# Spreading the next phase's H between the last two pairs of a phase, in a gather-and-sum trunk on one core

## What is computed

```python
def chunk_fn(args):
    hc, ic, gc = args                                # 128 tokens: h, 128 indices, 128 gates each
    act = jnp.einsum('cd,ckd->ck', hc, u_tab[ic])    # the "dots"
    return jnp.einsum('ck,ckd->cd', gc * jax.nn.gelu(act), v_tab[ic])   # the "sums"
```

## Time and profile before

| | us |
|---|---|
| median of 3 runs | 1794.7 (1791.46 to 1794.89) |
| the profiled execution | 1795.44 |
| its span in the trace | 1793.6 |

### The profile page before, as it was taken

How to read it: one execution, slowest core, us unless ns; L and a number is a source line. 1 busy time by engine, 2 the same in 40 slices (tenths; PEclk the granted TensorE clock), 3 DMA queues, 4 the chain that set the end, 5 groups by cost and what they waited for, 6 DMA issues and landing times.

```text
span 1793.6 us, 17530 instructions
## 1 busy us (share of the span) xinstructions
PE 1289.4 (72%) x5712; PEld 537.7 (30%) x5712; DVE 1126.5 (63%) x2528; ACT 663.7 (37%) x1983; POOL 623.6 (35%) x559
## 2 busy tenths in 40 slices
PE   3676545657876996897778789789987975545555
PEld 2364011112621333333336133353352620000000
DVE  8957989883558666435445766654453577676454
ACT  6524332222234328216423331751382243233222
POOL 5103334452232224324422322332332344444442
PEclk9897667889876998999989699899998986787676
DMA  7039899999997999999999899999999999999996
GB/s 313 1 123 397 337 423 413 409 407 419 422 423 304 409 423 419 425 423 421 422 423 423 337 367 425 421 367 420 423 378 411 422 349 421 410 417 413 420 422 282
DMA packets 88652, 685.29 MB, mean 382 GB/s; under 512 B 12144, under 2 KB 12272, under 8 KB 14320
## 3 DMA queue, kind: packets, MB, share of 16 engines
q0 software_dynamic: 73728, 536.90, 73.2%
q1 hardware_dynamic: 14832, 147.26, 19.7%
HBM read 683.08 MB, written 1.05 MB: 381 GB/s over the span
## 4 chain that ended last, share of the span: by engine, by line
DMA 35%; PE 33%; DVE 17%; ACT 6%; issue 5%; POOL 3%; SPq 1%; POOLq 0%; ACTq 0%; DVEq 0%
DMA ringmem<-experts,lay 24%; PE ps L437 11%; PE ps L407 10%; DMA wt<-w_qkv 7%; DVE ringmem L1068 6%; PE ps L447 4%; POOL ringmem L1039 3%; DMA wt<-w_o 2%; PE ps L422 2%; ACT lay L773 1%; DMA wt<-w_q 1%; ACT S L724 1%; PE ps L626 1%; PE ps L601 1%; PE ps L513 1%
## 5 line engine op out<-in xcount | busy, mean ns | idle before, releaser
L1039 POOL DMA_INDIRECT ringmem<-experts,lay x512 | 588.2, 1149 | 1084.4 <-PE ps L407 946.5
L407 PE MATMUL ps<-ringmem,S 128*32 128x512 f32 x2048 | 626.8, 774 | 393.8 <-ACT S L724 393.4
L1068 DVE CUSTOM_DVE_ANT_0 ringmem<-ringmem,Hrep 128x1024 f32<-128x1024 f32 x512 | 614.6, 1224 | 310.1 <-DMA ringmem<-experts,lay 300.6
L407 PEld LDWEIGHTS ps<-ringmem,S 128*32 128x32 f32 x2048 | 115.0, 128 | 817.4 <-ACT S L724 565.9
L719 ACT ACTIVATE gelus<-dots 128x2 f32<-128x2 f32 x256 | 51.6, 202 | 693.1 <-DVE dots L1068 692.2
L437 PE MATMUL ps<-wt,hT 128*128 128x512 f32 x576 | 256.2, 598 | 13.6 <-DMA wt<-w_qkv 13.5
L437 PEld LDWEIGHTS ps<-wt,hT 128*128 128x128 f32 x576 | 106.6, 190 | 163.3 <-issue 155.0
L715 ACT ACTIVATE S<-con,lay 128x32 f32<-128x32 f32 x512 | 134.3, 310 | 35.9 <-PE ps L407 35.8
L724 ACT ACTIVATE S<-S,gelus 128x32 f32<-128x32 f32 x512 | 136.9, 314 | 23.7
L447 PE MATMUL ps<-hT,wt 128*128 128x128 f32 x1024 | 119.8, 279 | 2.6 <-DMA wt<-w_q 1.5
L447 PEld LDWEIGHTS ps<-hT,wt 128*128 128x128 f32 x1024 | 117.1, 194 | 14.5 <-issue 6.3
(11 more groups left out here) (187 smaller groups left out, 1116.0 us busy)
## 6 DMA issues: line engine op xcount, KB each, us to landing
wt<-w_qkv SPq DMA_DIRECT2D x36, 2048.0 KB, 11.6
wt<-w_q SPq DMA_DIRECT2D x16, 2048.0 KB, 12.0
wt<-w_glu SPq DMA_DIRECT2D x5, 2048.0 KB, 12.5
ringmem<-experts,lay POOLq DMA_INDIRECT x512, 12.6
wt<-w_o SPq DMA_DIRECT2D x4, 2048.0 KB, 13.8
ringmem<-w_glu SPq DMA_DIRECT2D x3, 2048.0 KB, 17.1
gain<-gains SPq DMA_DIRECT2D x9, 512.0 KB, 15.0
area<-keys SPq DMA_DIRECT2D x4, 1024.0 KB, 9.6
```

The costliest lines, as they stand in the source:

```text
L407: last = pe.matmul(ps[TG * t:TG * (t + 1), half, :], S[:, u % 2, i, :], ring[:, (2 * u + i) % RING, D + half * 512:D + (half + 1) * 512], ...
L1039: pool.indirect_dma_start(ring[:, s % RING, :], None, experts[phase // NC], bass.IndirectOffsetOnAxis(ap=rows[:, phase % NC, j, n:n + 1], ...
L1068: last = v.tensor_tensor_reduce(ring[:, i, 0:D], ring[:, i, 0:D], Hrep[:, j, :], 1.0, 0.0, ALU.mult, ALU.add, dots[:, b, second:second + 1])
```

## The change

The same instructions run on every engine; only their order on PE, ACT and DVE is another, at the ends of phases 0, 1 and 2.
- PE puts two spread pieces (u = 0, 1) ahead of the sums of pair 63, two (u = 2, 3) ahead of those of pair 64, and four behind.
- ACT copies the first four pieces between its shares of pair 63 and of pair 64 (`g.at` at u = 0 runs up to pair 63, at u = 4 up to pair 64), the last four behind. The root comes behind all eight and behind ACT's share of the next pair 1.
- DVE does the dots of the next pair 1 ahead of the addition to `X`.

```diff
@@ PE, spread_h
                 pe.wait_ge(normed, norm_event(phase // NC, phase % NC, 1) + 1)
                 for u in range(2 * QUAD):
+                    if phase and u in (0, 2, 4):
+                        g.at(phase - 1, PAIRS_G - 2 + u // 2)
                     j, half = divmod(u, 2)
@@ PE, the phases
             layer0(0, 1)
-            g.at(0, PAIRS_G)
             spread_h(1)
             layer1(1, 0)
-            g.at(1, PAIRS_G)
             spread_h(2)
             layer1(2, 1)
-            g.at(2, PAIRS_G)
             spread_h(3)
             g.at(3, PAIRS_G)
@@ ACT, spread_h
-                if phase:
-                    act.wait_ge(dots_ready, PAIRS_G * phase)
                 for u in range(2 * QUAD):
                     j, half = divmod(u, 2)
+                    if phase and u in (0, QUAD):
+                        g.at(phase - 1, PAIRS_G - 1 + u // QUAD)
+                        act.wait_ge(dots_ready, PAIRS_G * phase - 1 + u // QUAD)
                     act.wait_ge(h_spread, 2 * QUAD * phase + u + 1)
                     act.copy(Hrep[:, j, half * 512:(half + 1) * 512],
                              ps[:, src[u % len(src)], :]).then_inc(hrep_ready, 1)
-                    if e is not None and u == 3:
-                        root(e)
+                if e is not None:
+                    g.at(phase, 1)
+                    root(e)
@@ DVE, peer_end
                 c = phase % NC
                 g.at(phase, PAIRS_G)
+                if phase + 1 < 2 * NC:
+                    g.at(phase + 1, 1)
                 v.wait_ge(v_pe, PAIRS_G * (phase + 1))
                 v.tensor_tensor(X[:, c, :], X[:, c, :], banks(0, 2), ALU.add).then_inc(peer_done, 1)
```

## The result

| | before | after |
|---|---|---|
| median of 20 runs | 1793.6 us | 1798.6 us |
| ratio, with its 95% interval | | 1.0024 (1.0014 to 1.0034) |
| span of the profiled execution | 1793.6 us | 1797.0 us |

The change makes the kernel 4.3 us slower (2.5 to 6.1, the ratio on 1794). I had forecast 8.6 us slower. The direction was right, the size was not, and the parts were further off than their sum: the ends of phases 0 and 1 cost nothing together, the end of phase 2 costs more than all I had given it.

The account below looks back on a forecast made before the run. Bound by a chain of waits shared between transfers (35%) and PE (33%), DVE third. Phase ends 0, 1 and 2 cost 4.6, 1.7 and 2.3 us, together +8.6 (3.7 to 13.4): 1803.3 us for a 1794.7 median, range 1790 to 1811.

Parts of the forecast that it names:

- The late root: Ends of phases 0 and 1: scaling starts 3.7 us behind the last spread piece, +3.6 us at each end.
- DVE full, so a shift passes on: Ends of phases 0 and 1: DVE is full behind the scaling, so nothing covers the +3.6 us per end.
- Rival 3: DVE has slack, only the next pair 1's release counts: together -1.2 us, 1793.5, no change; chance 0.07.
- The wait for ACT ahead of pair 64's sums: ACT's share of pair 64 stands behind the fourth copy, so PE idles about 2 us before those sums.
- The spread's end at the ends of phases 0 and 1: Last spread piece ends +1.0 us at phase 0's end and -1.9 at phase 1's, middles over the open clock.
- Rival 2: Two high-clock stretches at each of the first two ends, sums and pieces being mixed: 1792.8, no change; chance 0.17.
- The end of phase 2: PE is already full there: spread ends +2.3 us (0.2 to 4.3), all on the chain through waiting gathers.
- DVE's dots ahead: Next pair 1's dots move between idle stretches of DVE, done before pair 64's sums: nothing on the chain.
- The late gathers: Gathers behind the last two pairs go out up to 6 us later, but DMA is full, so nothing starves.
- rival 4: The late gathers starve the stream, 3 us more at each end: 1812 us; chance 0.05.

Follow-up runs that it names:

- the delayed root: Kernel before, with the root behind all copies and ACT's share of the next pair 1, plus ten unneeded ACT copies ahead of it; 18.6 us slower.
- the kernel with the end of phase 2 alone: Changed order kept only at the end of phase 2, ends of phases 0 and 1 as in the kernel before; 6.1 us slower than before.
- the inner root: Changed order at ends of phases 0 and 1, root behind the sixth copy, phase 2's end as before: 9.5 us faster; with DVE's dots behind, 5.2 faster.

## Why the prediction was right or wrong

- **The late root: right.** I had the scaling 3.7 us behind the spread's end; it came 3.5 behind at both ends (547.31 to 550.81). The kernel with the root put back was 6.6 us faster, of 6.8 expected. The single comparisons scatter (3.8, 6.6, about 9 and 0 us for two ends). At one end the spread's end moved by up to 2.2 us from profile to profile of one order, with the granted clock, which may be the reason but is not shown to be; that a shift passes on in full rests on the delayed root.
- **DVE full, so a shift passes on: right.** Rival 3 is excluded by the delayed root, and gathers of the next pair 1 that came 6.5 us earlier brought nothing that the time shows.
- **The wait for ACT ahead of pair 64's sums: right,** 1.82 us.
- **The spread's end at the ends of phases 0 and 1: wrong, the term that failed.** I took +1.0 and -1.9 between all at the low clock and one stretch of high clock. From the end of pair 64's dots to the spread's end it was 15.1 us before at both ends, and 12.1 and 11.7 after: -3.0 and -3.4. My list for the end of phase 0 gave 10.5 us to the first four pieces and the sums of pair 63, at the low clock; they took 5.7, because the high clock fell on them, some 7 us of it instead of 3.4. It is not one lucky profile: from the start of pair 64's second dot to the spread's end it takes 14.2 to 17.0 us in ten ends with the old order (five kernels), 16.0 in the mean, and 11.2 to 13.4 in ten ends with PE's and ACT's new order (five kernels), 12.6 in the mean. Rival 2, to which I gave 0.17, has twice the time at the high clock, and its arithmetic for these two ends (0.4 and -2.5) fits the measured 0.4 and 0.0 better than mine (4.6 and 1.7). Its reason, that sums and pieces are mixed, is not shown: the kernel with the end of phase 2 alone, which has the old order here, was granted the high clock at the same place, while PE had little to do (stretches as above).

```profile
528.60:535.60 7.00, 2.59 (x12) 0.52 (x12) 3.16 (x6) 1.90 (x8) 4.25 (x4) 0.99 1.01 420
```

  What the new order changes is that PE has four pieces to do in such a stretch. My middle took the clock only around the eight pieces of the old place.
- **The end of phase 2: right in sign, too small.** +2.3 (0.2 to 4.3) against 6.1. I priced the sums of pair 63 at 1.98, since the clock was high at that time before. In the new order it stayed low, so pieces and sums cost 3.8 and 3.6. And I misread: the 12 matmuls in 3.65 us there are the eight of pair 62 and four of pair 63. The sums of both stood back to back and took 4.77 us, so those of pair 63 added 1.1 us and not the 1.98 of my sum; with pieces on both sides they cost 3.6. The new wait was in my sum and came (1.82).
- **DVE's dots ahead:** nothing on the chain in the changed kernel, as forecast (they end at 540.3, the root at 550.6). With the inner root it was not settled.
- **The late gathers: right at the first two ends, wrong at the third.** At the end of phase 0 the DMA share stays at 1.01 until 548. At the end of phase 2 the first gathers behind pairs 63 and 64 go out at 1460.87 and 1468.53, where before they went out at 1456.01 and 1458.49, and the DMA share falls to 0.87 in 1460 to 1467 and 0.79 in 1467 to 1474.2. Up to the sums of the next pair 1 (1474.22) that is an estimated 2.9 us of missing transfers (what lacks to a share of 1, times the length); before, the share was 0.99 and 1.01 up to the same point (1467.54). I had looked at the end of phase 0 alone. That is rival 4's mechanism, to which I gave 0.05, at one end. How much of the 6.1 us goes through these gathers and how much through the late sums of the next pair 1 no run tells apart, for both are late by the same chain on PE.

The errors had opposite signs: 6 us too dear at the first two ends, 4 too cheap at the third. That the direction came out right is owed to this in part: by the intervals the first two ends together cost 0.4 us, and the loss is that of the third.

## What to carry to other kernels

When work is pulled forward on one engine, look at what it carries with it on the next: here the pieces were early by 3 us at two ends, and a square root set behind them took the same back. Give the dependent step its own place instead, and keep a waiting share of work ahead of copies that nobody awaits yet; with these two and the third end left alone the same idea gained 10 to 14 us, of which the share's place is the least certain part. And treat two ends that look alike apart: where the engine waits for transfers there is room between its steps, where it works off a queue there is none.

## What the runs showed of the hardware

- The sums of two pairs, which go to different columns of the array, take 4.77 us back to back at the low clock, one pair alone 3.63.
- Being busy alone did not bring PE the high clock: in the kernel with the end of phase 2 alone it was busy for 14.5 of 14.5 us at 0.50. And a high stretch was of one length in one place and of another in the next: 3.4 us at the end of phase 0 before (536.6 to 540.0) and 6.8 us at the end of phase 2 before (1454.8 to 1461.6), PE being busy throughout both, with pieces behind sums in both. In the three profiles with the changed end of phase 2 the clock stayed low for 11.5 us or more from the start of the sums of pair 62; in the others it rose 3 to 6 us after that start. The reason is open.
- With full-depth matmuls (128 rows, 128 columns) in PE's idle time its clock was at 1.00 for the whole stretch of 521 to 526 and at 0.96 in the ten us after. Four pieces then cost 3.8 us, against 6.6 at the low clock.
- The time of these kernels scatters by 10 to 15 us from run to run (the change's 20 runs lie between 1789 and 1804 us), and the same kernel came out 13.6 and 10.4 us faster than before in two sessions, between which the kernel before had itself moved from 1792.7 to 1800.4 us. A difference of 3 us between two of these orders is not certain.
